# Output projection of a hybrid decoder block: two column blocks against seven quadrant products

## The chip, the cores and the metric

The kernel is one program on one core of a Trainium2 chip. Time is the device time of the core in microseconds (us); the kernel before has a median of 1022.34 us over three runs. A core has TensorE (PE, matmuls, with its weight loads as PEld), VectorE (DVE), ScalarE (ACT), GpSimd (POOL), SyncE (SP, which here only issues DMAs) and 16 DMA engines. The engines run their own instruction streams in order and wait for each other by semaphores.

## The reference, cut to what matters

```python
merged = jax.nn.sigmoid(gate_r) * y_ret + jax.nn.sigmoid(gate_m) * y_m   # (512, 1024)
x = x + merged @ w_out                # w_out (1024, 1024): the output projection, then the residual
h = rms_norm(x, norm_ffn_w)           # 512 tokens
# router logits from h: 4 groups, 32 experts; top-1 group, top-2 experts in it, their weights
# 32 experts of (silu(xb @ w_gate[e]) * (xb @ w_up[e])) @ w_down[e], D = 1024, D_EXPERT = 512, float32
# y = x + weighted sum of the two experts of each token; final rms_norm
```

## The kernel before, in words

The 512 tokens stay in SBUF. The token mixers come first, the output projection after them, then the router, then the experts.

A projection before the experts is done in float32 precision by three float32r products: a value is split into a head (`wh` of the weights, `mrgTh` of the activations, copied by ScalarE) and a tail (`wl`, `mrgTl`, value minus head, by VectorE), and TensorE adds head times head, tail times head and head times tail. Weights pass through a ring of four entries (RING). An entry is 256 rows by 512 columns, one head copy on ScalarE (`mix_head`, 128x1024) and one subtraction on VectorE (`mix_tail`, 128x1024). The heads are issued three entries ahead (LEAD).

The stages before the output projection are the five wide projections done as seven quadrant products each (FAST), and four blocks of 512 columns (`B_WR`, `B_WM`, two each) for the two branches. The second `B_WM` block ends with the gated sum `mrg` (channels by tokens, 8 tiles of 128 by 512).

The output projection is two such blocks, `B_WO` and `B_WO + 1`: each has four steps j, each step 2 halves of 2 token tiles, 2 slices of 128 rows and 3 products, so 96 matmuls of 512 columns per block and 192 in all (line 674). VectorE adds each bank to the residual `x2` (line 1690).

After the last block every token tile of `x2` is turned (`turn_stream`, 8 transposes of 128x128 each), copied to `h2T` by VectorE and ScalarE, and multiplied with the router weights (`logits`, `logit_rows`). VectorE then does the routing. TensorE meanwhile does identity matmuls that nobody reads (`stay_awake`, line 924). GpSimd gathers the tokens of the first pair of experts from a copy of `x2` in DRAM (`x_scratch`, stored by SyncE, read by an indirect DMA into `xg`), TensorE turns them (line 631) and starts the first gate product (line 956).

The experts go in 16 pairs. Each pair needs 12 chunks of weights of 1 MB (8 for gate and up, 4 for down); 192 chunks in all pass through 22 places of 8 KB per partition (`raw_moe`, plus one `guest`). SyncE issues all loads in one written order. Places that mixers and projection still use are loaded later, each behind a wait. A place is loaded a second time when TensorE has used its first chunk (`wait_chunk_used`).

## Time and profile before

| what | us |
|---|---|
| median of three runs | 1022.34 (1022.29 to 1024.7) |
| the profiled execution | 1022.9 |
| its span (first to last instruction) | 1021.0 |
| TensorE busy | 996.3 |
| VectorE, ScalarE, GpSimd busy | 500.1, 323.9, 120.8 |
| output projection on TensorE | about 491 to 534.7 |
| stream turned and router logits | 534.7 to 543.3 |
| routing, up to the first gate product | 543.3 to 561.3 |
| experts and the end | 561.3 to 1021.0 |

The span starts at the first instruction; what lies around it is 1.9 us. A busy share of 98% on TensorE says little by itself: identity matmuls count as busy too. The chain of waits tells which engine an interval hangs on. A row of the windows gives the busy time of each engine in a stretch, then the granted clock, the share of the 16 DMA engines in use, and GB/s.

### The profile page before, as it was taken

The page shows a single profiled execution, that of the slowest core. Times are in us where ns is not written, and L with a number is a line of the kernel's source. Part 1 is how long each engine was busy: PE and PEld are TensorE (multiplying, and loading weights), DVE is VectorE, ACT ScalarE, POOL GpSimd, SP SyncE. Part 2 cuts the span into 40 slices and gives each one's busy share as a digit, 9 for nine tenths or more (in the row PEclk, how much of TensorE's full clock was granted, in tenths as well). Part 3 has the DMA queues.
Part 4 walks back from the last instruction along what each step waited for, and adds up shares of the span by engine and source line. Part 5 has one row for each costly group of instructions (what it writes and reads, how often), then busy time and mean ns, then how long its engine had stood idle before and what let it go on. Part 6 is the DMA issues. An engine that isn't in the chain of part 4 may idle for free.

```text
span 1021.0 us, 13126 instructions
## 1 busy us (share of the span) xinstructions
PE 996.3 (98%) x4917; PEld 644.4 (63%) x4917; DVE 500.1 (49%) x810; ACT 323.9 (32%) x531; POOL 120.8 (12%) x152
## 2 busy tenths in 40 slices
PE   8999999999999999999998999999999999999896
PEld 7888788889889988888885333333333333333332
DVE  6268646597778677735525123333223233332235
ACT  6344535586556557622213100000000000000012
POOL 0683077000000000000000000000000000000000
PEclk9999999999999999999999999999999999999999
DMA  9223231344334525162988899999999999999993
GB/s 331 83 83 126 92 114 21 83 125 145 66 91 113 185 42 205 43 213 90 422 307 357 348 420 420 420 420 420 420 420 420 421 420 420 420 421 421 421 414 146
DMA packets 63125, 269.28 MB, mean 264 GB/s; under 512 B 9488, under 2 KB 9680, under 8 KB 38360
## 3 DMA queue, kind: packets, MB, share of 16 engines
q1 hardware_dynamic: 57464, 257.32, 63.6%
q0 software_dynamic: 5344, 11.02, 4.9%
q8 instruction: 41, 0.67, 0.3%
q14 instruction: 20, 0.16, 0.0%
q10 hardware_dynamic: 256, 0.10, 0.0%
HBM read 268.41 MB, written 4.20 MB: 267 GB/s over the span
## 4 chain that ended last, share of the span: by engine, by line
PE 72%; SPq 17%; DVE 5%; DMA 3%; ACT 2%; issue 1%; DVEq 0%; ACTq 0%
PE pj L674 23%; PE pj L854 18%; PE pj L956 12%; SPq L575 11%; PE pj L982 6%; SPq L572 6%; PE cb L631 3%; DMA raw_moe<-in_w_up_dram 3%; PE cb L992 2%; PE cb L993 1%; DVE mkT L1758 1%; DVE wl L1494 1%; PE cb L723 1%; PE cb L695 1%; ACT wh L1136 1%
## 5 line engine op out<-in xcount | busy, mean ns | idle before, releaser
L956 PE MATMUL pj<-raw_moe,xT 128*64 128x512 f32 x1016 | 227.6, 595 | 4.2 <-DMA raw_moe<-in_w_up_dram 2.4
L1494 DVE TENSOR_TENSOR wl<-raw_mix,wh 128x1024 fp32r<-128x1024 f32 x116 | 146.2, 1262 | 130.9 <-ACT wh L1136 130.6
L1970 DVE TENSOR_TENSOR x<-x,cb 128x512 f32<-128x512 f32 x120 | 77.0, 683 | 190.2 <-PE cb L993 190.2
L956 PEld LDWEIGHTS pj<-raw_moe,xT 128*64 128x64 f32 x1016 | 72.1, 137 | 140.8 <-issue 140.8
L1136 ACT ACTIVATE wh<-raw_mix 128x1024 fp32r<-128x1024 f32 x116 | 122.4, 1057 | 111.4 <-PE pj L674 68.5
L982 PE MATMUL pj<-raw_moe,hf 128*64 128x512 f32 x512 | 116.7, 598 | 1.6 <-ACT hf L1440 1.6
L982 PEld LDWEIGHTS pj<-raw_moe,hf 128*64 128x64 f32 x512 | 34.6, 136 | 67.2 <-issue 67.0
L1445 ACT ACTIVATE yh<-pj,now 128x512 fp32r<-128x512 f32 x32 | 20.4, 683 | 157.6 <-PE cb L993 143.6
L1440 ACT ACTIVATE hf<-cb 128x512 f32<-128x512 f32 x16 | 9.6, 598 | 146.3 <-PE cb L631 146.3
L992 PE MATMUL cb<-yh,hot 128*128 128x512 f32 x124 | 55.2, 445 | 0.0
L674 PE MATMUL pj<-wh,hTh 128*128 128x512 f32 x128 | 50.8, 397 | 1.7 <-DVE hTl L1525 0.7
L1975 DVE TENSOR_TENSOR xT<-cb,nwc 128x512 f32<-128x512 f32 x32 | 21.9, 687 | 58.0 <-PE cb L631 58.0
L674 PE MATMUL pj<-wl,hTh 128*128 128x512 f32 x128 | 49.9, 390 | 0.0
L674 PE MATMUL pj<-wh,hTl 128*128 128x512 f32 x128 | 49.9, 390 | 0.0
L993 PE MATMUL cb<-yl,hot 128*128 128x512 f32 x124 | 49.2, 397 | 0.0
L1436 ACT ACTIVATE sg<-pj,now 128x512 f32<-128x512 f32 x16 | 11.0, 688 | 100.7 <-PE pj L956 90.0
L992 PEld LDWEIGHTS cb<-yh,hot 128*128 128x128 f32 x124 | 23.6, 190 | 29.0 <-issue 26.2
L854 PE MATMUL pj<-wh,hTh 128*128 128x512 f32 x96 | 39.0, 406 | 0.7 <-DVE mva L1811 0.7
L854 PE MATMUL pj<-wl,hTh 128*128 128x512 f32 x96 | 37.6, 391 | 0.0
L854 PE MATMUL pj<-wh,hTl 128*128 128x512 f32 x96 | 37.4, 390 | 0.0
L854 PE MATMUL pj<-hTh,wh 128*128 128x256 f32 x128 | 36.5, 285 | 0.0
L1986 DVE SCALAR_TENSOR_TENSOR sg<-pj,now,sg 128x512 f32<-128x512 f32 x16 | 12.0, 751 | 49.5 <-PE pj L956 49.5
(397 smaller groups left out, 1858.5 us busy)
## 6 DMA issues: line engine op xcount, KB each, us to landing
raw_moe<-in_w_gate_dram SPq DMA_DIRECT2D x64, 1024.0 KB, 26.7
raw_moe<-in_w_down_dram SPq DMA_DIRECT2D x64, 1024.0 KB, 26.7
raw_moe<-in_w_up_dram SPq DMA_DIRECT2D x63, 1024.0 KB, 26.0
raw_mix<-in_w_in_dram SPq DMA_DIRECT2D x31, 1024.0 KB, 5.3
raw_mix<-in_w_in_dram POOLq DMA_DIRECT2D x10, 512.0 KB, 5.8
raw_mix<-in_w_ret_branch_dram SPq DMA_DIRECT2D x4, 1024.0 KB, 5.8
raw_mix<-in_w_mlstm_branch_dram SPq DMA_DIRECT2D x4, 1024.0 KB, 5.5
raw_mix<-in_w_out_dram SPq DMA_DIRECT2D x4, 1024.0 KB, 5.1
```

The lines of the kernel that those rows point to most:

```text
L572: sp.dma_start(weights_of(m)[:, :, :].rearrange("p (f c) n -> p f (c n)", f=2), w_down[0][e].rearrange("(a p f) n -> p a f n", a=2, f=2)[: ...
L575: sp.dma_start(weights_of(m)[:, :, :], (w_gate, w_up)[kind][0][e].rearrange("(a p k) n -> p a k n", a=2, k=4)[:, half, :, :]).then_inc(lan ...
L631: return nc.tensor.transpose(o, i, kc[0:k, K_IDENT:K_IDENT + k])
L674: m = nc.tensor.matmul(pj[:, i, :], lhsT, rhs, start=k == 0 and n == 0, stop=k == KD - 1 and n == 2)
L854: m = nc.tensor.matmul(o, lhsT, rhs, start=u in (U_11, U_21, U_T1) and k == 0 and c == 0 and n == 0, stop=k == 3 and n == 2, skip_group_ch ...
L956: mm = nc.tensor.matmul(pj[a * CAP:(a + 1) * CAP, up, :], xT[:, 4 * half + k, a * CAP:(a + 1) * CAP], weights_of(m + a)[:, k, :], start=ha ...
L982: mm = nc.tensor.matmul(pj[a * CAP:(a + 1) * CAP, 2 + c, :], hf[:, 2 * half + f, a * CAP:(a + 1) * CAP], weights_of(m + a)[:, 2 * f + c, : ...
L992: nc.tensor.matmul(bank, hot[:, t * P:(t + 1) * P], yh[:, c * 512:(c + 1) * 512], start=begin, stop=False)
L993: return nc.tensor.matmul(bank, hot[:, t * P:(t + 1) * P], yl[:, c * 512:(c + 1) * 512], start=False, stop=True)
L1136: nc.scalar.activation(wh[:, q % RING, :, :], entry_source(q), ACT.Copy).then_inc(wh_ok, 1)
L1494: V.tensor_tensor(wl[:, q % RING, :, :], entry_source(q), wh[:, q % RING, :, :].bitcast(F32), ALU.subtract).then_inc(wl_ok, 1)
L1970: V.tensor_tensor(part, part, cb[:, 2 + g % 2, :], ALU.add).then_inc(c_add, 1)
```

## The change

The output projection is written as seven products of quadrants, as the FAST projections already are. A quadrant of the activations is 512 channels by 256 tokens, one of the weights 512 by 512. With seven products in place of eight there are 7 x 2 x 4 x 3 = 168 matmuls of 512 columns. The sums that this needs are all on VectorE: four of activations (`out_part_sum`), eight of half weight quadrants (`out_weight_sum`), and 14 additions into `x2` (two for each product; ScalarE copies the `U_T1` product out first). Heads and tails of activations are now seven parts of 128x1024. The upper left weight quadrant and the upper right one get their own loads into places 12 and 13 of `raw_moe`; the right one is loaded there and again into `raw_mix`, so w_out comes in five loads of 1 MB instead of four. The expert chunks of places 12 and 13 move behind the projection. The turning of token tiles 0 and 1 and half of the logits move between the last products. The places 10, 11, 18, 19 of `raw_moe` change addresses among themselves.

```diff
-                    if b == B_WO:
-                        pe.wait_ge(mgl_ok, 2 * j + 2)
+            def out_half(u, s):
+                if u == U_11:
+                    pe.wait_ge(*out_free(s, 0))
+                if u == U_21:
+                    pe.wait_ge(*out_free(2 + s, 0))
+                if u == U_22:
+                    pe.wait_ge(tr_h, 2 * KD + s + 1)
+                if u in (U_T2, U_T3, U_T4):
+                    pe.wait_ge(*out_free(s, (U_T2, U_T3, U_T4).index(u) + 1))
+                if s == 0:
+                    pe.wait_ge(mgl_ok, (1, 3, 4, 5, 6, 2, 7)[u])
...
+            for u in range(PRODUCTS):
+                for s in range(2):
+                    out_half(u, s)
+                    if u == U_T3:
+                        turn_stream(s)
+                    if u == U_T4 and s == 0:
+                        pe.wait_ge(wrt_ok, 1)
+                        logits(0)
+            turn_stream(2)
+            logit_rows(0)
+            turn_stream(3)
             logits(1)
-            logit_rows(0)
             logit_rows(1)
...
+                    if b == B_WM + 1 and j >= 2:
+                        out_weight_sum(U_T3, j - 2)
+                    if b == B_WM + 1 and j == 3:
+                        out_weight_sum(U_T2, 0)
+                        out_weight_sum(U_T2, 1)
...
+            for x in range(2 * PRODUCTS):
+                if x in (9, 10):
+                    upper_right_last(x - 9)
+                if x in (11, 12):
+                    lower_right_last(x - 11)
+                    stream_turned(x - 11)
+                if x == 13:
+                    lower_left(0)
+                if x == 0:
+                    out_part_tail(2)
+                if OUT0 + x + LEAD < ENTRIES:
+                    mix_tail(OUT0 + x + LEAD)
+                if x == 0:
+                    out_part_sum(2)
+                    out_part_tail(3)
+                    out_part_sum(3)
+                if x in (1, 2):
+                    first_sum(x - 1)
+                if x in (3, 4):
+                    out_part_tail(x + 1)
+                if x == 5:
+                    second_sum(0)
+                    second_sum(1)
+                    out_part_tail(6)
+                if x in (6, 7):
+                    out_weight_sum(U_T4, x - 6)
+                if x == 9:
+                    router_weights()
...
-            moe_chunk(13, 0, False)
-            moe_chunk(14, 0, False)
...
-            for m in (2, 3, 5, 6):
+            for m in (2, 3, 5):
                 moe_chunk(m, 0, False)
-            sp.wait_ge(mgl_ok, KD)
-            moe_chunk(7, 0, False)
+            sp.wait_ge(mgl_ok, 7)
             moe_chunk(8, 0, False)
...
             for t in range(TT):
-                sp.wait_ge(free[t], free_of(t, BLOCKS - 1))
+                sp.wait_ge(*tile_ready(t))
                 sp.dma_start(x_dram[t * P:(t + 1) * P, :], x2[:, t, :]).then_inc(st_in, 16)
+                if t == 1:
+                    sp.wait_ge(wl_ok, out_entry(U_T4, 1) + 1)
+                    moe_chunk(14, 0, False)
+                    sp.wait_ge(*out_full(U_T3, 1))
+                    for m in (15, 17, 11, 12):
+                        moe_chunk(m, 0, False)
```

The first place is VectorE at the end of the second `B_WM` block and at the start of the projection. `wl` rows are tails of weight entries, `sgm` rows read and free the four banks, `mrg` rows are the gated sum, `mrgTl` rows are tails of it. Before:

```order
L1494 TENSOR_TENSOR wl<-raw_mix_114,wh 128x1024
L1683 TENSOR_TENSOR sgm<-pj,sgm 128x512 x4
L1696 TENSOR_TENSOR mrg<-mrg,sgm 128x512 x2
L1587 TENSOR_TENSOR mrgTl<-mrg,mrgTh 128x512
L1696 TENSOR_TENSOR mrg<-mrg,sgm 128x512
L1587 TENSOR_TENSOR mrgTl<-mrg,mrgTh 128x512
L1696 TENSOR_TENSOR mrg<-mrg,sgm 128x512
L1587 TENSOR_TENSOR mrgTl<-mrg,mrgTh 128x512 x2
L1494 TENSOR_TENSOR wl<-raw_mix_114,wh 128x1024
```

The same place now (`e5f`, `s2f` and `e3f` are sums of activations, `e5l` a tail):

```order
L1637 TENSOR_TENSOR wl<-raw_mix_126,wh 128x1024
L1759 TENSOR_TENSOR raw_mix_124<-raw_mix_124,raw_mix_125 128x1024
L1759 TENSOR_TENSOR raw_moe_109<-raw_moe_110,raw_mix_125 128x1024 x2
L1866 TENSOR_TENSOR sgm<-pj,sgm 128x512
L1868 TENSOR_TENSOR mrg<-mrg,sgm 128x512
L1866 TENSOR_TENSOR sgm<-pj,sgm 128x512
L1868 TENSOR_TENSOR mrg<-mrg,sgm 128x512
L1866 TENSOR_TENSOR sgm<-pj,sgm 128x512
L1868 TENSOR_TENSOR mrg<-mrg,sgm 128x512
L1866 TENSOR_TENSOR sgm<-pj,sgm 128x512
L1868 TENSOR_TENSOR mrg<-mrg,sgm 128x512
L1736 TENSOR_TENSOR e5f<-mrg 128x1024
```

Three weight sums now stand between the last tail of `B_WM` and the row that frees the first bank, each bank's `mrg` stands right behind its `sgm`, and sums and tails of parts (the last row is the first of them) follow before the ring's next tail.

The second place is VectorE in the middle of the projection, between the second product and the fifth. Before, between two tails of weight entries, stood the four additions of the first block:

```order
L1494 TENSOR_TENSOR wl<-raw_mix_113,wh 128x1024
L1690 TENSOR_TENSOR x_112<-pj,x_112 128x512 x4
L1720 TENSOR_TENSOR wrt<-wrt,nwc 128x8x36
L1721 MEMSET wrt 128x8x28
L1722 TENSOR_TENSOR fold<-kc 128x64
L1494 TENSOR_TENSOR wl<-raw_mix_113,wh 128x1024
```

Now:

```order
L2092 TENSOR_TENSOR x_123<-x_123,pj 128x512 x2
L1770 TENSOR_TENSOR mrgTl<-mrg,mrgTh 128x4x256
L1637 TENSOR_TENSOR wl<-raw_moe_109,wh 128x1024
L1759 TENSOR_TENSOR raw_moe_110<-raw_moe_109,raw_mix_126 128x1024
L1637 TENSOR_TENSOR wl<-raw_mix_124,wh 128x1024
L1759 TENSOR_TENSOR raw_moe_110<-raw_moe_109,raw_mix_126 128x1024
L2097 TENSOR_TENSOR x_123<-x_123,t1c 128x512 x2
L1637 TENSOR_TENSOR wl<-raw_mix_124,wh 128x1024
L2102 TENSOR_TENSOR x_123<-x_123,cb 128x512 x2
L2108 TENSOR_TENSOR x_123<-x_123,pj 128x512
L1637 TENSOR_TENSOR wl<-raw_moe_110,wh 128x1024
```

Line 2108 is the row that frees the first bank for the product `U_T3`; everything above it comes first.

The third place is SyncE's queue around the stores of `x_scratch`. Before:

```order
L575 DMA raw_moe_102<-in_w_up_dram 128x2048
L604 DMA x_scratch<-x_112 128x1024 x4
L575 DMA raw_moe_101<-in_w_up_dram 128x2048
L575 DMA raw_moe_103<-in_w_up_dram 128x2048
L575 DMA raw_moe_104<-in_w_up_dram 128x2048
L572 DMA raw_moe_105<-in_w_down_dram 128x2048
```

Now:

```order
L672 DMA x_scratch<-x_123 128x1024 x2
L616 DMA raw_moe_110<-in_w_gate_dram 128x2048
L616 DMA raw_moe_111<-in_w_gate_dram 128x2048
L616 DMA raw_moe_113<-in_w_up_dram 128x2048
L613 DMA raw_moe_107<-in_w_down_dram 128x2048
L616 DMA raw_moe_108<-in_w_gate_dram 128x2048
L672 DMA x_scratch<-x_123 128x1024 x2
L616 DMA raw_moe_112<-in_w_up_dram 128x2048
```

Five chunks of 1 MB now stand between the stores of tiles 0 and 1 and those of tiles 2 and 3, which the gather waits for.

## Rows read from the trace of the kernel before

**Rows 1.** The page's first line.

```profile
span 1021.0 us, 13126 instructions
```

**Rows 2.** Chain of waits, 484 to 580: start, length, what.

```profile
483.93 50.78 PE pj L674 x224
534.71 1.93 PE cb L631 x16
536.63 1.94 PE pj L631 x16
538.57 3.60 PE cb L900 x32
542.17 1.16 PE cb L909 x8
...
552.81 4.14 PE pj L924 x6
...
558.01 1.91 PE pj L924 x4
559.92 0.48 PE cb L631 x4
...
561.27 13.97 PE pj L956 x64
```

**Rows 3.** Windows: busy time of each engine, granted clock, DMA share, GB/s.

```profile
495.00:507.00 12.00, 12.00 (x55) 9.94 (x54) 5.59 (x7) 3.77 (x5) 0.00 (x0) 1.00 1.01 419
507.00:519.00 12.00, 12.00 (x55) 9.94 (x54) 5.62 (x9) 2.12 (x2) 0.00 (x0) 1.00 0.82 329
...
555.00:561.00 6.00, 5.87 (x48) 3.23 (x46) 1.50 (x7) 1.49 (x2) 0.53 (x1) 0.96 0.68 235
561.00:567.00 6.00, 5.73 (x28) 2.43 (x30) 0.72 (x2) 0.00 (x0) 1.03 (x1) 1.00 0.28 67
...
579.00:900.00 321.00, 318.80 (x1445) 124.02 (x1441) 99.43 (x158) 30.12 (x47) 16.62 (x36) 1.00 1.01 420
```

**Rows 4.** TensorE's timeline, 950 to 962, with the idle time before each.

```profile
951.14 3.65 PE L956 MATMUL pj<-raw_moe,xT 128*64 128x512 f32 x16 [1.32 <-DMA raw_moe<-in_w_gate_dram]
956.13 3.66 PE L956 MATMUL pj<-raw_moe,xT 128*64 128x512 f32 x16 [1.33 <-DMA raw_moe<-in_w_up_dram]
```

**Rows 5.** VectorE's timeline, 484 to 545.

```profile
486.93 1.22 DVE L1494 TENSOR_TENSOR wl<-raw_mix,wh 128x1024 fp32r<-128x1024 f32 x1 [4.21 <-ACT wh L1136]
488.08 1.28 DVE L1683 TENSOR_TENSOR sgm<-pj,sgm 128x512 f32<-128x512 f32 x2
...
497.36 2.36 DVE L1494 TENSOR_TENSOR wl<-raw_mix,wh 128x1024 fp32r<-128x1024 f32 x2 [0.25 <-ACT wh L1136]
```

**Rows 6.** Groups of VectorE by line and form, 300 to 491.

```profile
L1654 DVE TENSOR_TENSOR raw_mix<-raw_mix,raw_mix 128x1024 f32<-128x1024 f32 x13 | 15.8, 1219 | 0.0
```

**Rows 7.** ScalarE's timeline, 533 to 543.

```profile
538.19 1.07 ACT L1407 ACTIVATE squares<-x 128x1024 f32<-128x1024 f32 x1
539.13 0.21 ACT L1407 ACTIVATION_READ_ACCUMULATOR squares<-x 128x1 f32 x1
539.23 0.60 ACT L1412 ACTIVATE h2T<-pj 128x512 f32<-128x512 f32 x1
```

**Rows 8.** DMA issues: number, KB each, median us from issue to landing.

```profile
x_scratch<-x SPq DMA_DIRECT2D x4, 512.0 KB, 7.2
...
xg<-x_scratch,tok_now POOLq DMA_INDIRECT x14, 8.3
...
xg<-x_scratch,tok_tab POOLq DMA_INDIRECT x2, 4.1
```

**Rows 9.** SyncE's timeline, 430 to 640.

```profile
531.38 4.40 SPq L604 DMA_DIRECT2D x_scratch<-x  x4
...
556.02 9.34 SPq L572 DMA_DIRECT2D raw_moe<-in_w_down_dram  x2
```

**Rows 10.** GpSimd's timeline, 540 to 625.

```profile
554.13 1.40 POOL L2171 DMA_INDIRECT xg<-x_scratch,tok_tab  x1 [183.70 <-DVE cnt L2020]
```

**Rows 11.** Window of the routing stage.

```profile
543.40:561.30 17.90, 15.31 (x96) 7.54 (x96) 11.68 (x49) 3.37 (x6) 1.40 (x1) 0.90 0.87 338
```

More of the change, by code:

```diff
@@ L421, in entry_used, with out_entry, out_place, out_full @@
             return pair_used, 3 * F0 + PRODUCTS * len(FAST) + 3 * (b - B_WR) + j + 1
+        def out_entry(u, v):
+            return OUT0 + 2 * u + v
+        out_slot = {U_11: 12, U_T1: 13, U_T2: 12, U_T4: 13}
+        OUT_SUM = {U_T1: 1, U_T3: 4, U_T2: 6, U_T4: 11}
+        ROW_SUM = (3, 8, 9, 10)
+        def out_place(u):
+            return raw_moe[out_slot[u]] if u in out_slot else raw_mix[slot_of(2 * B_WO + (U_T3, U_22, U_21).index(u))]
+        def out_full(u, s):
+            if u in (U_T1, U_22):
+                return tr_ps, 2 * KD + (2 if u == U_22 else 0) + s + 1
+            if u == U_21:
+                return full[2 + s], full_of(2 + s, B_WM + 1) + 1
+            return full[s], full_of(s, B_WM + 1) + (U_11, U_T2, U_T3, U_T4).index(u) + 1
+        def out_free(s, n):
+            return free[s], free_of(s, B_WM + 1) + n
+        def tile_ready(t):
+            return out_free(t % 2, 2 + t // 2 * 2)
+        def stream_bank(t, half):
+            return cb[:, 2 * t + half, :] if t < 2 else pj[:, 6 - 2 * t + half, :]
         def half_before(x):
@@ L476, in mix_chunk @@
                     w, c0 = w_in[0], IN_COLS[b]
-                else:
-                    w, c0 = (w_ret, w_mlstm, w_out)[(b - B_WR) // 2][0], 512 * (b % 2)
+                elif b < B_WO:
+                    w, c0 = (w_ret, w_mlstm)[(b - B_WR) // 2][0], 512 * (b % 2)
                 m = n - 2 * B_WR
@@ L488, in mix_chunk @@
                     sp.wait_ge(wl_ok, fast_entry(len(FAST) - 1, U_T4 if m else U_T3, 1) + 1)
+                if n >= 2 * B_WO:
+                    half, c0, w = ((0, 512), (1, 512), (1, 0))[n - 2 * B_WO] + (w_out[0],)
                 sp.dma_start(raw_mix[slot_of(n)][:, :, :],
@@ L767, in block_of @@
             def block_of(b):
[L768 removed]
+                act = (hTh, hTl) if b < B_WR else (retTh, retTl) if b < B_WM else (mixTh, mixTl)
                 if b == B_RK:
@@ L885, in turn_stream @@
             def turn_stream(t):
-                pe.wait_ge(free[t], free_of(t, BLOCKS - 1))
+                pe.wait_ge(*tile_ready(t))
+                if t == 0:
+                    pe.wait_ge(tr_l, 2 * KD + 4)
+                if t == 2:
+                    for i in (2, 3):
+                        pe.wait_ge(*out_free(i, 1))
                 for half in range(2):
-                    bank = cb[:, 2 * t + half, :] if t < 2 else pj[:, 2 * t + half - TT, :]
                     for k in range(4):
-                        m = turn(bank[:, k * P:(k + 1) * P], x2[:, t, 512 * half + k:512 * (half + 1):4])
+                        m = turn(stream_bank(t, half)[:, k * P:(k + 1) * P], x2[:, t, 512 * half + k:512 * (half + 1):4])
                     m.then_inc(h2T_ps, 1)
@@ L1313, in block_of @@
                         root(3 + b - B_WR, 8)
+                    if b == B_WM + 1 and j < 2:
+                        out_part_head(j)
             def fast_evict(p, u, s):
```

287 lines of the change are left out of this document (214 added, 73 removed).

## The prediction, blind

> **What bounds the kernel now.** I read the page, the chain of waits, the windows and the timelines of single engines, in that order. The span is 1021.0 us [rows 1]. From 484 to 543.3 the chain is TensorE without a break: the projection, 16 + 16 transposes, the logits, the logit rows; each piece starts where the last ends [rows 2]. 224 matmuls take 50.78 us, so one takes 0.2267 us, and the 192 of the projection take 43.5 us: it starts at 534.7 - 43.5 = 491.2. The reader should see that VectorE is less than half busy there (5.6 of 12 us) [rows 3]. From 543.3 the chain is small VectorE work and identity matmuls, and at 559.92 the first gathered tokens are turned [rows 2].
>
> From 579 to 900 TensorE is busy, but the DMA engines are also full, at 420 GB/s [rows 3]. A chunk of 1.049 MB then takes 2.50 us, a pair's twelve 30.0 us. TensorE needs less than that per pair and eats up its lead of 22 places; at 951 and 956 it waits for chunks, 1.3 us each [rows 4]. So both limits meet near the end. To finish earlier the kernel must start the experts earlier **and** the stream of chunks must get ahead. The slack of the stream is one hole: at 561 to 567 the DMA engines are used at 0.28 (67 GB/s), because all places are full and the next load waits for a first use [rows 3]; SyncE's row with two issues from 556.02 lasts 9.34 us, so the second is issued near 565.0 [rows 9].
>
> **TensorE's work.** 24 matmuls fewer, 24 x 0.2267 = -5.4 us. Transposes, logits and rows are as many as before; moving them costs nothing by itself.
>
> **VectorE's work.** A 128x1024 tail costs 1.14 us in a row of them (2.36 for two, less 1.22) [rows 5]; a 128x1024 sum has the same length, 1219 ns [rows 6]. A 128x512 addition costs 0.60 in a row (1.28 for two, less 0.68) [rows 5]. Strided 4x256 forms are not in the trace as tails; I take them at the 128x1024 price, nearest in size. The engine's queue, followed through the changed order:
>
> - The last `B_WM` tail starts at 486.93, the next instruction could start at 488.08 [rows 5]. Three weight sums are now in front of the four banks: 3 x 1.14, so 491.5. The first bank is free at 492.2 instead of before 491.2: TensorE waits **1.1**.
> - The gated sum now stands behind each bank and waits for its own predecessor: 4 x (0.60 + 0.60 + 0.14) = 5.4, to 496.9. One part sum and one tail later, at 499.3, the second product may start; TensorE is done with the first at 492.3 + 5.4 = 497.7. It waits **1.7**.
> - Third product: its first weight tail is seventh in the queue, 496.9 + 7 x 1.14 = 505.0, about when TensorE comes (499.4 + 5.4 = 504.8); the next tail is behind a bank addition. Together **0.8**.
> - The product `U_T3` needs bank 0, freed by the first `U_T2` addition. From 496.9 to its end stand 3 part sums, 5 part tails, 9 weight tails, 2 weight sums and 9 additions: 19 x 1.14 + 9 x 0.60 = 27.1, with waits for its own results 524.3. TensorE could be there at 499.4 + 4 x 5.44 + 0.8 = 522.0. It waits **2.3**.
>
> VectorE thus works without a pause from 486.9 to about 528, and waits of 5.9 us take the place of 5.4 saved.
>
> **The end of the projection.** From 524.3: four halves of 2.72 (10.9), turns of tiles 0 and 1 (1.9), half the logits (1.8): 538.9. Then turn, rows, turn (0.97 + 0.3 + 0.97): 541.1. The second half of the logits waits for ScalarE, which after tile 2 is turned (539.9) does copy, square, copy: 0.5 + 1.2 + 0.6 [rows 7], 542.3; TensorE waits 1.2, then 1.8 for the logits and 0.9 for copy and rows: 545.3 where it was 543.33 [rows 2]. **Routing starts 2.0 us later.** Bounds: if ScalarE's chain overlaps the turn fully, 1.2 less; if each 4x256 tail cost a tenth more, 0.8 more.
>
> **SyncE's queue.** Chunks of places 12 and 13 came early; now nothing is issued from about 492 until the seventh part tail. Its place in VectorE's queue is 14 x 1.14 + 4 x 0.60 after 496.9, near 515.5. Before, the engines were full or at 0.82 in this time [rows 3]. Behind it wait 17 chunks (42.5 us), 2.1 MB of stores (5) and the token row (0.6): about 48 us from 517.6, so full to about 566. Before, the last of these had landed soon after 561 (share 0.68, then 0.28) [rows 3]. Two things hang on it.
>
> The **stores** of tiles 2 and 3 stand behind five chunks (12.5 us). In the trace the four stores follow one another within 4.40 us [rows 9] and land 7.2 us after issue [rows 8]. Now tile 3's is issued near 539.8 and lands near 552. The gather comes at 554.13 + 2.0 = 556.1 [rows 10]: covered, but only by 4 us. Without the stalls of VectorE this would be the next bound.
>
> The **gather** runs beside a full queue. The first two, beside an emptying queue, landed after 4.1 us (median), the other fourteen, with the stream full, after 8.3 [rows 8]. At 554.13 + 4.7 (the first of the two is the longer; the window's half empty share speaks for no more) TensorE was still in its identity matmuls, which end at 559.92 [rows 2]: 0.9 us of cover. Now 556.1 + 8.3 = 564.4 against 559.92 + 2.0 = 561.9: **2.5 to 2.7 more**. Bounds: 0 (4.1 as before) and 4 (9.5 us of backlog ahead of it).
>
> The Trainium skill (DMA: Bandwidth & Descriptors, Queues, rings and completion order) says that a DMA engine alternates between queue rows packet by packet. By that rule the gather shares with the chunks and doesn't stand behind them. The rows with 8.3 us agree with sharing; were it one line, the sum would be 1.5 us larger.
>
> **Experts.** The first gate product begins at 561.27 + 4.7 = 566.0, the first place is free near 569.7, after the queue has run dry (566), so the stream starts as much later as TensorE does. Both limits that met at 951 move by the same amount, nothing absorbs it. The fifth load of w_out (2.5 us) falls into the hole before 517 and costs nothing; without the hole it would be 2.5 us of the stream.
>
> **Sum.** -5.4 + 5.9 + 1.2 + 0.3 for the order of the last rows = +2.0; gather +2.7; **+4.7** in all. The profiled execution has 1022.9 us (1.9 more than its span) and would become 1027.6; on the median of 1022.34 the same step gives **1027.0**.
>
> **Rivals.**
>
> 1. *The gather doesn't feel the queue.* Everything else holds, +2.0: 1024.4. For it: the backlog is only 10 us deep, not 26. Against: 8.3 in all fourteen busy cases. Chance 0.18.
> 2. *VectorE keeps up and TensorE's 5.4 us arrive.* Then routing would start 4 us earlier. It doesn't end there: tile 3's store lands near 550, the gather is 3.6 slower, and the chunks still need 48 us from the seventh tail, which comes some 3 us earlier; the first gate product comes 0 to 1 us earlier, 1021.8. Chance 0.12. It is faster by over 0.3%, at 1017, only if the chunks also get through early: the hole between 492 and 517 must then not exist. It decides at the point where the seventh part tail is done before 505. Together with all that I overlooked, 0.05.
> 3. *The clock falls in the gather's wait.* In the routing stage the granted clock has a mean of 0.90, and three doubled identity matmuls take 4.14 us where two later take 1.91 [rows 2, 11]. Before that fall TensorE had small work with gaps. Now it waits 2.6 us for the gather; if the clock is at 1.2 GHz in the first 4 us of the gate product, 1.7 more: 1028.7. Chance 0.15. The Trainium skill (TensorE: Matmul & The Clock Gate, Part 1) has the gate follow recent activity; this trace shows one such fall, none after a wait as short as this.
> 4. *Slower still:* 4x256 forms a tenth dearer and the stores behind the gather, 1030. Chance 0.05.
>
> Forecast itself: 0.45. A change of 0.3% is 3.07 us; this is about what a measurement of this kernel tells from none. Above 1025.4 lie the forecast's cases but for its lower edge, 3 and 4; between, the lower edge, 1 and most of 2. Slower 0.70, same 0.24, faster 0.06. Range 1021.8 to 1030.2; the likeliest case alone 1025.3 to 1029.
>
> **What would show it.** Right: VectorE busy over 90% from 487 to 528; TensorE idle about 1, 1.7, 0.8 and 2.3 us at the starts of the products 1, 2, 3 and 6; DMA share near 0 for ten microseconds around 510, then full to 566; first `xg` gather landing after 8 us and TensorE idle before line 705's `xg` rows. Wrong: a projection of 38 us without gaps; a gather of 4 to 5 us; the DMA engines full before 515; or a steady stream that catches up later and leaves the end where it was.

## The result and the profile after

The changed kernel takes 1033.27 us (median of five, 1029.1 to 1033.86) where the kernel before takes 1022.34: 10.9 us more. The ratio is 1.0085, with a 95% interval of 1.006 to 1.0109. A second series of the same kernel (`e18_after_again`) gave 1033.22 against 1023.11, ratio 1.0095 (1.0079 to 1.011). Two of the five executions took only 1029.1 and 1029.5, so the means, 1031.9 and 1023.2, are 8.6 us apart, less than the medians. So it is slower, as forecast, but by about twice the 4.7 us of the forecast, and the median is above its range; those two executions are inside it.

The profiled execution is the median one. The page's first line, to [rows 1]:

```profile
span 1031.4 us, 13137 instructions
```

The chain of waits from 484 on (start, length, what), to [rows 2]:

```profile
498.19 0.85 DVE mrgTl L1770
499.25 1.22 DVE wl L1637
...
524.27 4.61 PE pj L1015 x12
...
533.56 2.77 PE pj L1015 x12
536.33 1.88 PE cb L976 x16
538.21 2.96 PE pj L1015 x12
...
546.85 0.65 PE cb L985 x4
...
558.29 9.69 DMA xg<-x_scratch,tok_tab
...
569.71 15.64 PE pj L1071 x64
```

Four readings. The part from 491 to 524 has turned from TensorE into VectorE work: VectorE is busy for 40.5 of the 41 us from 487 to 528. The first half of product 6, twelve matmuls, takes 4.61 us from 524.27 while a like one later takes 2.77. The gather of the first tokens is now in the chain, 9.69 us long. The first 64 gate matmuls take 15.64 us; before, 13.97 [rows 2]. They start at 569.71 in place of 561.27.

The windows (busy time of PE, PEld, DVE, ACT, POOL, then granted clock, DMA share, GB/s), to [rows 3, 11]:

```profile
503.00:518.00 15.00, 14.80 (x64) 11.52 (x63) 15.00 (x16) 10.00 (x11) 0.00 (x0) 1.00 0.09 22
518.00:531.00 13.00, 11.24 (x46) 8.78 (x45) 11.05 (x16) 4.48 (x7) 0.00 (x0) 0.87 1.00 413
...
556.00:562.00 6.00, 5.63 (x22) 2.35 (x22) 3.48 (x18) 1.46 (x2) 1.41 (x1) 0.50 1.02 419
562.00:568.00 6.00, 3.57 (x37) 1.91 (x36) 0.00 (x0) 0.03 (x1) 0.00 (x0) 0.93 0.83 336
568.00:574.00 6.00, 5.50 (x22) 2.50 (x24) 1.29 (x2) 0.00 (x0) 1.03 (x1) 0.72 0.11 31
```

VectorE has no pause from 503 to 518, and the DMA engines stand nearly still there (22 GB/s; 329 in 507 to 519 before, [rows 3]). From 518 to 566 they are full (in the row from 562 on, 1.0 up to 566, then 0.65 and 0.28 in the last two us). TensorE's granted clock is below 1 in three places of this part: 0.87 in 518 to 531 means 3.4 of the 13 us at 1.2 GHz, 0.50 in 556 to 562 all six (before: 0.90 over the whole routing stage), and 0.72 in 568 to 574 another 3.4 us, now under the first gate products.

The timelines of TensorE and GpSimd around the waits, to [rows 2, 10]; in brackets the idle time before and who ended it:

```profile
492.28 0.50 PE L1015 MATMUL pj<-wh,mrgTh 128*128 128x512 f32 x1 [1.04 <-DVE sgm L1866]
...
524.27 0.50 PE L1015 MATMUL pj<-wh,mrgTh 128*128 128x512 f32 x1 [1.76 <-DVE x L2108]
...
568.11 1.21 PE L705 MATMUL cb<-kc,xg 128*128 128x128 f32 x8 [2.54 <-DMA xg<-x_scratch,tok_tab]
```

```profile
558.29 1.41 POOL L2432 DMA_INDIRECT xg<-x_scratch,tok_tab  x1 [187.78 <-DVE cnt L2281]
```

And SyncE's, to [rows 9]: the load of the second round is issued at 575.5 (560.19 + 15.28, end of a row with two issues) where it was issued at 565.4.

```profile
515.57 1.46 SPq L613 DMA_DIRECT2D raw_moe<-in_w_down_dram  x2
...
537.08 5.16 SPq L672 DMA_DIRECT2D x_scratch<-x  x2
...
560.19 15.28 SPq L613 DMA_DIRECT2D raw_moe<-in_w_down_dram  x2
```

At the end of the experts nothing has been made up; the waits for chunks of [rows 4] stand 10 us later:

```profile
961.58 3.65 PE L1071 MATMUL pj<-raw_moe,xT 128*64 128x512 f32 x16 [1.62 <-DMA raw_moe<-in_w_gate_dram]
966.54 3.65 PE L1071 MATMUL pj<-raw_moe,xT 128*64 128x512 f32 x16 [1.31 <-DMA raw_moe<-in_w_up_dram]
```

### The profile page after: what moved, and what is told of

It reads as the page before. It is cut to its first block, busy times and chain, and to the rows that moved or that the text cites. A ratio compares the mean times of both kernels' runs of the same rounds, so it can differ in the third digit from the quotient of the medians.

```text
span 1031.4 us, 13137 instructions
## 1 busy us (share of the span) xinstructions
PE 998.3 (97%) x4893; PEld 641.2 (62%) x4893; DVE 526.6 (51%) x833; ACT 333.2 (32%) x538; POOL 120.8 (12%) x152
## 4 chain that ended last, share of the span: by engine, by line
PE 67%; SPq 17%; DVE 8%; DMA 4%; issue 2%; ACT 2%; DVEq 0%; POOLq 0%; POOL 0%; ACTq 0%
PE pj L926 18%; PE pj L748 18%; PE pj L1071 12%; SPq L616 11%; PE pj L1097 6%; SPq L613 6%; DMA raw_moe<-in_w_up_dram 3%; PE cb L705 3%; DVE wl L1637 2%; PE cb L1107 2%; PE cb L1108 1%; PE pj L1015 1%; DMA xg<-x_scratch,tok_tab 1%; DVE mkT L1923 1%; ACT wh L1251 1%
## 5 line engine op out<-in xcount | busy, mean ns | idle before, releaser
L1637 DVE TENSOR_TENSOR wl<-raw_mix,wh 128x1024 fp32r<-128x1024 f32 x114 | 143.7, 1261 | 116.8 <-ACT wh L1251 116.4
```

What stands on the lines that cost most here:

```text
L1637: V.tensor_tensor(wl[:, q % RING, :, :], entry_source(q), wh[:, q % RING, :, :].bitcast(F32), ALU.subtract).then_inc(wl_ok, 1)
```

## Experiments

All were timed in five rounds beside the kernel before, whose median was 1023.1 to 1023.4 in these series. "Rows end" is the end of the last logit row, where routing starts (543.3 before, 547.5 after).

### Pauses of TensorE and its clock: e1_awake

The changed kernel with small matmuls of ones, which nobody reads, ahead of three waits:

```diff
+            def filler(n):
+                for _ in range(n):
+                    nc.tensor.matmul(cb[:, 3, 0:P], onesq[:, :], onesq[:, :], start=True, stop=True)
             def out_half(u, s):
+                if s == 0:
+                    filler({U_11: 4, U_21: 5, U_T3: 7}.get(u, 0))
```

> The changed kernel, with 4, 5 and 7 small matmuls that nobody reads (128x128 of ones) put ahead of TensorE's waits for the products 1, 2 and 6. Nothing else moves. Theory A (TensorE's waits in the projection make the clock fall to 1.2 GHz at 525.3, which costs 1.9 us): the granted clock stays at 1.00 from 500 to 550, the half product after 524.3 takes 2.7 us instead of 4.6, the routing starts near 545.7 instead of 547.5, the time is 1.5 to 2 us shorter (1031 to 1032) and the five runs lie closer together. Rival (the fall is not tied to these waits, or comes elsewhere then): the fall is still there and the time is that of the changed kernel, 1029 to 1034.

Measured: 1029.87 us (1029.13 to 1031.61), ratio 1.0071 (1.0057 to 1.0085). The median is 3.4 us below that of the changed kernel, more than the 1.5 to 2 us expected, although the matmuls do nothing. The ratios of the two kernels lie closer (1.0085 and 1.0095 without the matmuls) and their intervals overlap. What speaks for an effect is the single times: seven of the nine of the changed kernel, in two series, are above 1031.8, and none of these five is. The profiled execution is the shortest of the five. Its chain:

```profile
524.24 3.02 PE pj L1022 x12
...
545.24 0.65 PE cb L985 x4
...
556.68 8.89 DMA xg<-x_scratch,tok_tab
...
567.31 13.97 PE pj L1078 x64
```

Product 6 starts at the same moment as without them (524.2), so VectorE's queue is as long as it was; only the speed behind the wait has changed: 3.02 in place of 4.61. Rows end at 545.9, 1.6 us earlier. The gather takes 8.9 us, the gate products run at full speed. The edit does not touch that place, so these 1.7 us at the gate are not shown to be its work.

### The late queue and the gather: e4_quiet, e5_before_late

e4_quiet is the changed kernel with four chunks (places 15, 17, 18, 19) held back until the first gather has landed:

```diff
-            for m in (16, 18, 19, 20):
-                moe_chunk(m, 0, False)
             sp.wait_ge(lg_ps, 2)
             moe_chunk(GUEST, 0, False)
+            sp.wait_ge(gat, 16)
+            for m in (16, 18, 19, 20):
+                moe_chunk(m, 0, False)
```

> The changed kernel, but the four chunks of places 15, 17, 18, 19 are issued only after the first gather has landed; token row and guest chunk go before. Theory A (the gather is slow, 9.7 us instead of 4.7, because the queue is full beside it): the queue is dry near 556, the gather issued at 558.3 lands near 563, the gate product starts after the identity matmuls, near 567 instead of 569.7, and since the four chunks now fill the hole before the first reuse of a place, the end moves by the same 2.5 to 4 us, to 1029 to 1031. Rival B (the stream decides): four chunks 7 us later put the stream off, the time is 1035 or more. Rival D (the gather is slow for another reason, its store or the indirect addressing): it still takes over 8 us and the time is that of the changed kernel or worse.

Measured: 1032.92 us (1032.34 to 1033.72), ratio 1.0098 (1.0083 to 1.0114). The gather, issued at 556.6, landed after 4.6 us, TensorE did not wait for it, and the first gate product began at 563.9, 5.8 us earlier than in the changed kernel (1.6 of it because the clock did not fall in the projection of this execution). The time is between the cases expected, 1029 to 1031 and 1035 or more. Nothing of the gain reached the end: TensorE now waits for chunks eight times, 9.3 us in sum, from 868.7 on (three times and 4.0 us in the changed kernel).

```profile
868.67 3.65 PE L1072 MATMUL pj<-raw_moe,xT 128*64 128x512 f32 x16 [0.56 <-DMA raw_moe<-in_w_gate_dram]
873.63 3.65 PE L1072 MATMUL pj<-raw_moe,xT 128*64 128x512 f32 x16 [1.30 <-DMA raw_moe<-in_w_up_dram]
```

So the full queue is what makes the gather long, and holding chunks back only moves the price into the stream.

e5_before_late is the kernel before, projection and all, with the two chunks whose places the change takes for w_out issued behind the stores:

```diff
-            moe_chunk(13, 0, False)
-            moe_chunk(14, 0, False)
...
-            for m in (16, 18, 19, 20):
+            for m in (13, 14, 16, 18, 19, 20):
```

> The kernel before, with the chunks of places 12 and 13 (two loads of 1 MB) issued behind the stores of the tokens instead of before the projection: SyncE's part of the change alone, in small. Theory A: the queue is full until about 561, so the first gather at 554.1 takes 8 us or more instead of 4.7 and lands near 562.5; the gate product starts 2.5 to 3.5 us later than 561.3, maybe with a fall of the clock behind the wait (1.7 more); time 1025 to 1027. Rival (the two chunks fill the hole of the DMA engines at 561 to 567 and nobody waits for them): time as before, 1022.3.

Measured: 1028.32 us (1027.58 to 1028.53), ratio 1.0048 (1.0034 to 1.0062). Rows end at 543.4 as before, and yet 4.9 us are lost against its kernel before, 1.3 us past the upper end of what was expected:

```profile
554.00 8.64 DMA xg<-x_scratch,tok_tab
...
564.75 15.83 PE pj L954 x64
```

The gather takes 8.6 in place of 4.7 us, TensorE waits 3.8 for it, and its clock is at 1.2 GHz after that wait: 15.83 in place of 13.97. Two megabytes later in one queue cost half of what the whole change does. The matmuls at the gate are slow here behind a projection without a pause, so the clock's fall there does not need the waits of the projection.

### VectorE's weight sums: e3_light, e7_pool6

e3_light cuts each of the eight weight sums to one column. The products then use wrong weights, and the routing that follows from them led to a second round of the experts (28 later gathers in the trace in place of 14), so its total (1514.98 us) says nothing and only the trace up to the first gate product is read.

```diff
-                V.tensor_tensor(dst, one, two, ALU.add).then_inc(sum_ok, 1)
+                V.tensor_tensor(dst[:, :, 0:1], one[:, :, 0:1], two[:, :, 0:1], ALU.add).then_inc(sum_ok, 1)
```

> The changed kernel with the eight weight sums cut to one column of each row, so the products work on wrong weights; what is left out is 8 x about 1 us of VectorE. Theory A (VectorE's queue makes TensorE wait 4.9 us and the clock falls after it): no waits over 0.5 us in the projection, U_T3 starts near 518.5 instead of 524.3, no fall of the clock there, routing starts near 539.8 instead of 547.5. The end does not follow in full: the seventh part tail comes only 3.4 us earlier, so chunks fill the DMA engines until about 563, the gather takes 9 to 10 us and the first gate product starts near 562 to 563; time 1024 to 1026, still not below the kernel before. Rival B (the stream of chunks decides alone, whatever TensorE does): first gate product earlier, but the time within 2 us of the changed kernel, 1030 or more. Rival C (TensorE's time was all): 1033.3 - 7.7 = 1025.6 without the gather's share, and below 1022 if the gather is short.

Measured: no wait in the projection, rows end at 541.6 (1.7 earlier than before, 1.8 later than expected). But the gather, issued at 552.4, landed after 9.2 us, TensorE waited 3.5 for it, and the first gate product began at 563.7, still 2.4 later than before:

```profile
561.70 1.96 PE L705 MATMUL cb<-kc,xg 128*128 128x128 f32 x8 [3.52 <-DMA xg<-x_scratch,tok_tab]
```

Seven products that VectorE's weight sums do not hold up would have given nothing here, with SyncE's order as it is.

e7_pool6 moves six of the eight sums (`U_T3`, `U_T2`, `U_T4`) to GpSimd, which is idle then:

```diff
+            for u in (U_T3, U_T2, U_T4):
+                for v in range(2):
+                    pool_weight_sum(u, v)       # two adds of 128x512 each
             pool.wait_ge(st_in, 16 * TT)
```

> The changed kernel with the weight sums of T3, T2 and T4 on GpSimd (six of eight), nothing else. VectorE is 6 x 1.2 us freer, so products 2, 3 and 6 no longer wait; if the fall of the clock at 525.3 follows these waits it is gone, the last row ends at 542.5 to 544 (547.5 in the changed kernel), the gather still takes 8 to 9.5 us beside the queue, TensorE's clock falls once more in the gather's wait, and the time is 1027 to 1029. If TensorE's clock falls anyway, it is 1030 to 1033.

Measured: 1030.22 us (1030.0 to 1030.96), ratio 1.0071 (1.0058 to 1.0084), above the 1027 to 1029 expected. No fall of the clock in the projection, rows end at 545.0 where 542.5 to 544 was expected. That is 0.9 earlier than with VectorE alone and no fall; 6 x 1.14 = 6.8 us of work had left VectorE. VectorE's and GpSimd's timelines of this run tell where it went:

```profile
501.95 1.22 DVE L1641 TENSOR_TENSOR wl<-raw_moe,wh 128x1024 fp32r<-128x1024 f32 x1
503.08 0.68 DVE L2083 TENSOR_TENSOR x<-x,pj 128x512 f32<-128x512 f32 x1
503.68 1.94 DVE L1641 TENSOR_TENSOR wl<-raw_moe,wh 128x1024 fp32r<-128x1024 f32 x1
...
506.14 1.71 DVE L1641 TENSOR_TENSOR wl<-raw_mix,wh 128x1024 fp32r<-128x1024 f32 x1
507.78 2.31 DVE L1772 TENSOR_TENSOR e3l<-e3f,e3h 128x1024 fp32r<-128x1024 f32 x1
510.01 2.31 DVE L1641 TENSOR_TENSOR wl<-raw_mix,wh 128x1024 fp32r<-128x1024 f32 x1
```

```profile
503.25 7.99 POOL L2430 TENSOR_TENSOR raw_moe<-raw_moe,raw_mix 128x512 f32<-128x512 f32 x4 [15.40 <-DVE wl L1641]
```

While GpSimd adds, four subtractions on VectorE take 1.94, 1.71, 2.31 and 2.31 us in place of 1.22: 3.4 us go back. The account is closed with it: the gated sum starts at 489.6 in place of 491.6 (three sums fewer ahead of it, but the tail before it now waits for ScalarE's head), two sums further on are 2.3 us more, and 2.0 + 2.3 - 3.4 = 0.9. The additions that read a bank (0.68) are not longer. The Trainium skill (SBUF — State Buffer, Who interferes with whom) says that a VectorE instruction with two SBUF inputs contends with a GpSimd instruction that reads SBUF. The rows agree: GpSimd's additions are longer too, 2.0 us each (7.99 for four) where two at 479.76 took 3.46 together. They don't show that one stands still for the whole of the other.

### The clock in the gather's wait: e10_late_wake, e13_pool_wake, e15_wake

Small matmuls ahead of the turn of the gathered tokens, in three kernels: ten in e5_before_late (e10), eight in e7_pool6 (e13), ten in the changed kernel (e15).

```diff
             stay_awake(2)
+            wake(10)
             first_gate(0)
```

> The kernel before with the chunks of places 12 and 13 issued behind the stores (its run alone gave 1028.3, first gate product at 564.8, clock at 1.2 GHz from 561.7 for 6.8 us) and ten small matmuls ahead of the wait for the gather. If the clock that falls in that wait is part of the price, it stays at 2.4 GHz at the first gate products and the time is 1026 to 1027; the rest, 3 to 4 us over the kernel before, is then the gather beside the queue. If the late chunks cost only by their stream, the time stays at 1028.

Measured: 1027.29 us (1026.35 to 1028.25), ratio 1.0037 (1.0023 to 1.0051), against 1.0048 without them. The wait for the gather is 1.95 in place of 3.81; the clock still falls, but 2.7 us later, and is at 1.2 GHz for 3.4 us in place of 6.8. The first gate product stays where it was (564.7), since the gather takes 9.0. The time is 0.3 above the 1026 to 1027 expected; the gain of 1 us is within the intervals of the two kernels, so it is not shown.

> The same with eight small matmuls ahead of the gather's wait: against the run with the six sums on GpSimd alone it parts the clock in that wait from the gather beside the queue. If the clock is priced as elsewhere, it gives back 1.5 to 2 us, so 1025.5 to 1027; the queue's 4 us stay. If the gather alone decides, the two are equal.

Measured: 1029.5 us (1027.94 to 1030.34), ratio 1.0058 (1.0045 to 1.0071); the gather took 9.8, the wait for it was still 3.2, the gate matmuls took 15.45. The 1025.5 to 1027 expected did not come: against e7_pool6 it is 0.7 us less, not told apart from none, and the clock fell with the eight matmuls too, 3.1 us later and for 3.4 us in place of 6.8.

> The changed kernel with ten small matmuls ahead of the wait for the gather alone; the projection is as in the changed kernel, its clock fall at 525 too. Of the 3.4 us that the matmuls ahead of products 1, 2 and 6 gave (1033.3 to 1029.9), this tells which part belongs to the gate's clock: if the fall at the first gate products costs 1.7 us, the time is 1031 to 1032; if the price was all in the projection, it stays at 1033.

Measured: 1031.5 us (1029.67 to 1034.37), ratio 1.0086 (1.0072 to 1.0099). The times spread over 4.7 us. The profiled one is a short one (1029.9). Its projection has the waits of the changed kernel, with nothing edited there, and no fall of the clock:

```profile
524.31 0.50 PE L1015 MATMUL pj<-wh,mrgTh 128*128 128x512 f32 x1 [1.74 <-DVE x L2109]
...
566.34 1.20 PE L705 MATMUL cb<-kc,xg 128*128 128x128 f32 x8 [1.45 <-DMA xg<-x_scratch,tok_tab]
```

```profile
518.00:531.00 13.00, 11.26 (x53) 9.07 (x52) 11.00 (x16) 5.03 (x8) 0.00 (x0) 1.00 1.00 405
```

The fall in the projection, then, happens in some executions and not in others. e4_quiet's trace, with the same projection, has none either. So of the four traces with this projection and no matmuls in its waits, two have the fall (the changed kernel's and e18_after_again's) and two do not; the profiled run of e1_awake alone does not tell its effect from chance.

### Which wait, and is it by chance: e17_fill6, e18_after_again

```diff
-                    filler({U_11: 4, U_21: 5, U_T3: 7}.get(u, 0))
+                    filler({U_T3: 7}.get(u, 0))
```

Of e1_awake's matmuls, e17 keeps only those ahead of product 6 (the diff is against e1_awake), and it has the ten at the gather of e15_wake; e18 is the changed kernel without an edit.

> The changed kernel with seven small matmuls ahead of product 6 (the wait of 1.76 us at 524.3) and ten ahead of the gather's wait; products 1 and 2 wait as before. If the clock in the projection falls for the wait of product 6 alone, the times are 1028.5 to 1030.5 with none above 1032. If it falls for the sum of the waits, some of the five runs are still at 1032 to 1034, as with the ten alone.

Measured: 1030.69 us (1029.14 to 1031.31), ratio 1.007 (1.0056 to 1.0083). No time above 1031.4; with the ten alone, three of the six that e15 gave were. Rows end at 546.0, and the clock stays up in the projection though the waits ahead of products 1 and 2 are as long as in the changed kernel. That points at the wait ahead of product 6, but it is not shown: the intervals of e15 and e17 overlap, and e15's own trace has no fall either. The clock fell at the gate here, ten matmuls or not.

> The changed kernel once more, without an edit. Its five times stood at 1029.1, 1029.5, 1033.3, 1033.6 and 1033.9, and the trace with the clock's fall at 525.3 is one of the long ones. If that fall happens in some executions and not in others, the times part again in two groups about 4 us apart, and a trace of the short group shows no fall in the projection and the last row at 545.8 to 546. If the fall is always there, the cause of the two groups is elsewhere and a short trace shows it too.

Measured: 1033.22 us, four times from 1031.88 to 1034.3, ratio 1.0095 (1.0079 to 1.011). The short group did not come back, so the two groups are not shown on this kernel again. The granted clock over each execution says something of them: the two short ones of the first series had a mean of 0.994, its three long ones 0.988 to 0.991, and the four here 0.990 to 0.993. They differ in how long the clock was down. The kernel before spreads with it too, from 1021.98 us at 0.997 to 1024.78 at 0.993 in the series beside e1_awake, so not all of the spread belongs to the change. The profiled time, the longest, has the fall once more (row one), and the one at the gate (row two):

```profile
524.99 4.42 PE pj L1015 x12
...
570.73 15.65 PE pj L1071 x64
```

### How much is the queue: e11_less, e12_before_less

In both, half of each of the chunks m = 14 to 19 is not loaded in the first round (3.1 MB), and their products read the loaded half twice, so the output isn't the reference's. e11 is e1_awake with this edit, e12 the kernel before.

```diff
-                    sp.dma_start(weights_of(m)[:, :, :], ...[:, half, :, :])
+                    ks = slice(0, 2 if not used and m in (14, 15, 16, 17, 18, 19) else 4)
+                    sp.dma_start(weights_of(m)[:, ks, :], ...[:, half, ks, :])
```

> The changed kernel with the small matmuls ahead of products 1, 2 and 6 (1029.9 without more), and with half of each of the chunks m = 14 to 19 left out in the first round (3.1 MB less, about 8.6 us of the queue at 363 GB/s; the products of the second pair of experts read the loaded half twice, so the output is not the reference's). If the queue that VectorE's sums leave late is what delays the experts, the queue has run dry by about 559, the gather takes 5 to 6 us in place of 8.9, the first gate product starts at 562.5 to 564 in place of 567.3 and the time is 1024 to 1026. If the stream of chunks sets the end by its bytes alone, the time falls by the whole 8.6, to 1021. If neither, it stays at 1029 to 1030.

> The same halves left out in the kernel before (output not the reference's). Its queue is dry at 554 and its slots are full when the first gate product starts, so if it has no shortage of chunks the time stays within 1 us of 1022.5; if its stage of experts is set by the stream's bytes, it falls by up to 8.6 us, to 1014 to 1015. That result is the scale against which the run of the changed kernel with these halves left out is read.

Measured: e11 1025.56 us (1024.34 to 1027.27, eleven runs), ratio 1.0025 (1.0016 to 1.0034); e12 1023.2, ratio 0.9999 (0.999 to 1.0008). So the bytes alone are worth nothing in the kernel before, and 4.3 us in the changed one (1029.87 - 1025.56). The intervals of e11_less and e1_awake do not overlap. The windows of e11 and its chain:

```profile
550.00:556.00 6.00, 3.80 (x37) 1.65 (x36) 5.02 (x22) 0.20 (x1) 0.00 (x0) 1.00 1.02 422
556.00:562.00 6.00, 5.52 (x48) 3.21 (x47) 2.27 (x12) 1.49 (x2) 1.41 (x1) 1.00 0.61 219
```

```profile
562.79 13.97 PE pj L1079 x64
```

The DMA engines run dry while the gather is under way; issued at 556.5, it landed at 560.8, under the identity matmuls, and the gate product starts at 562.8 instead of 567.3.

### Does a later start carry over: e16_before_fill

```diff
             stay_awake(2)
+            wake(18)
             first_gate(0)
```

> The kernel before with eighteen small matmuls (0.22 us each) ahead of the turn of the gathered rows: nothing else moves, and the first gate product starts 4 us later, at 565.3. In the traces so far the span is the start of the first gate product plus 459.7 to 460.1 where the clock stays up, whichever kernel it is; if the experts' stage is an unbroken stream that begins there, this run takes 1027 us. If the stream has slack to make up the delay, it takes 1023 to 1025.

Measured: 1026.39 us (1026.28 to 1028.14), ratio 1.0035 (1.0021 to 1.0049), 3.3 us over its kernel before. In the profiled execution (1028.14, the longest; it is 0.9 late from the start of the program on, where the clock was down for 3.4 us) the first gate product is at 566.3 and the span 1026.3: 5.0 and 5.3 us later than in the kernel before. The stage of experts has no slack. All traces but e3_light's beside one another, us:

```
kernel                first gate product   span     difference   clock at the gate
before                561.3                1021.0   459.7        full
e12_before_less       561.4                1021.5   460.1        full
e16_before_fill       566.3                1026.3   460.0        full
e11_less              562.8                1022.5   459.7        full
e1_awake              567.3                1027.3   460.0        full
e15_wake              567.9                1028.0   460.1        full
e10_late_wake         564.7                1026.0   461.3        fell
e13_pool_wake         567.1                1028.4   461.3        fell
e17_fill6             567.5                1028.8   461.3        fell
e7_pool6              566.7                1028.4   461.7        fell
e18_after_again       570.7                1032.4   461.7        fell
after                 569.7                1031.4   461.7        fell
e5_before_late        564.8                1026.6   461.8        fell
e9_pool_awake         565.9                1027.9   462.0        fell
e14_pool_wake_hold    563.6                1025.9   462.3        full, 2 chunks held back
e4_quiet              563.9                1030.5   466.6        full, 4 chunks held back
```

The time is the start of the first gate product plus 460, plus 1.3 to 2.0 where the clock is down there, plus what the stream lacks where chunks come late.

### Attempts at a better version: e9_pool_awake, e14_pool_wake_hold

e9 is e7_pool6 with the matmuls of e1_awake and eight at the gather. e14 is e13_pool_wake with places 18 and 19 issued after the gather has landed.

> The changed kernel with three edits: the weight sums of T3, T2 and T4 go to GpSimd (six of the eight that VectorE does), products 1, 2 and 6 have small matmuls of ones ahead of their waits, and eight more stand ahead of the wait for the gather. If the loss were made in the projection (VectorE's sums and the clock), the last row would end at about 543 as in the kernel before, the first gate product would start at 562 to 563 and the time be 1023 to 1025. If most of it is SyncE's order (chunks issued late, the gather behind a full queue), the row ends at 543 to 545, but the gather still takes 8 to 9 us beside the chunks, the first gate product starts at 565 to 567, and the time is 1027 to 1029.

Measured: 1027.97 us (1027.26 to 1029.72), ratio 1.0045 (1.0031 to 1.0059). No wait in the projection at all, rows end at 545.3, gather 8.0: the second of the two cases foreseen.

> The same again with two of the six late chunks (places 18 and 19, 2.1 MB, 5.8 us of the queue) issued only when the gather has landed. By the queue's account the gather lands 2 to 4 us sooner and the first gate product starts at 561 to 563; if two chunks held back don't leave the experts short, the time is 1022.5 to 1025, no worse than the kernel before. If the bytes then come too late, as with four held back, TensorE waits for chunks in the experts by about what it won, and the time is 1027 to 1030.

Measured: 1028.65 us (1027.79 to 1029.64), ratio 1.0057 (1.0044 to 1.0069). The gather landed after 6.4 and the gate product began at 563.6, but TensorE then waited for chunks five times, 5.8 us (three and 3.8 in e13). No version with the seven products came to the kernel before. The hole of the DMA engines from 503 to 518 is common to all of them, and the bytes missed there have to come when the gather wants the engines, or later, when the experts want them. A version in which SyncE has something to load in that hole was not run.

## Why the prediction was wrong in size

The direction and the path were right; three terms were too small, one of them taken as nothing, and a fourth stood only as an unlikely rival. Of the 10.4 us of span:

| step | forecast | trace |
|---|---|---|
| rows end, clock up | +2.0 | +2.6 (e1_awake, e15_wake) |
| clock falls at product 6 | not named | +1.6 (547.5 against 545.9) |
| gather behind its cover | +2.7 | +4.2 (8.4 less 4.2) |
| clock at the first gate products | rival 3: +1.7, chance 0.15 | +2.0 (461.7 against 459.7) |
| sum | +4.7 | +10.4 |

**TensorE's work, VectorE's work.** These held. The waits ahead of products 1, 2, 3 and 6 were forecast as 1.1, 1.7, 0.8 and 2.3 us and are 1.04, 1.39, 0.20 and 1.76, together 4.4 in place of 5.9. That product 6, forecast at 524.3, starts at 524.27 is VectorE's queue read rightly; that the loss before it comes out as 5.8 is partly luck, since the 120 matmuls of the first five products took 28.6 us and not 27.2, about what the waits fell short. VectorE worked without a pause, and the loss ate the saving of 24 matmuls.

**The end of the projection.** It was to be 545.3 and was 547.5. With the clock up it is 545.9, so the working was 0.6 short: the four halves took 11.5 us (3.02, 2.78, 2.77, 2.96) and not 10.9; ScalarE's wait was 0.91, not 1.2, but a further 0.48 stood ahead of the rows. (Walked piece by piece, the prediction's own terms end at 545.0; the 545.3 comes from its sum.) The other 1.6 is the step that failed first: after 524.3 I priced every matmul at 0.2267 us, as if TensorE's clock did not care for the pauses put before it. I had looked for the clock in the gather's wait alone (rival 3). In the profiled execution it fell at 525.3, 1.0 us after the wait of 1.76. e15_wake and e4_quiet show that it doesn't happen each time. With matmuls in the wait of product 6 no trace of three has the fall (e1_awake, e11_less, e17_fill6) and no time of e1_awake and e17_fill6 is above 1031.7; that fits the waits as its cause, and does not prove it.

**SyncE's queue.** The hole was forecast from 492 to 515.5 and full engines to 566; SyncE issues again at 515.57, and the engines are full until 566. e12_before_less shows that the kernel before had room for these bytes, e11_less that the changed one has not.

**The gather.** Its issue came 4.2 us late, as rows end did. I took 8.3 us, the median of the fourteen gathers in the steady stream [rows 8], as if all had it; in the trace of before they lie between 7.9 and 9.7. This one took 9.69. This term is the second step that failed, 4.2 in place of 2.7. Beside a full queue the first gather took 8.0 to 9.8 in the eleven traces that have one. Less the cover, that is just past the upper bound of 4 that I gave. In the changed kernel and in e5_before_late it lands just when the engines fall idle (share 0.65 in 566 to 567, 0.28 in 567 to 568, landed at 567.97), which looks like standing in line. It isn't: in e7_pool6 the engines are full to 567 and the gather lands at 564.5 after 8.9 us, in e9_pool_awake at 564.2 after 8.0. The length hangs on whether the engines are full, little on how much stands ahead. The Trainium skill's rule (DMA: Bandwidth & Descriptors, Queues, rings and completion order), that an engine alternates between the queues it has work for, agrees with these traces.

**Rival 3** was right and got a chance of 0.15, because the trace of before showed "none after a wait as short as this". It had no such wait at all (its longest for chunks are 1.3 us): absence was read as evidence. Of the nine traces of timed kernels with a wait of 1.67 us or more for the gather, with matmuls ahead or not, eight took 15.1 to 15.8 us for the first 64 gate matmuls; e1_awake, with 1.71, took 13.97, and so did e15_wake with 1.45 (13.98). The length of the wait is not all of it: e9_pool_awake, with 1.67, took 15.67. In e1_awake and e15_wake the clock had already fallen and come back under the identity matmuls of the routing, where it costs nothing; in the six of the eight that are neither the changed kernel nor its second run it had stayed up there until after 561. The granted clock of e1_awake (row one) and e9_pool_awake (row two):

```profile
556.00:562.00 6.00, 6.00 (x38) 2.61 (x36) 2.44 (x12) 1.49 (x2) 1.41 (x1) 0.56 1.01 416
556.00:562.00 6.00, 5.52 (x52) 3.49 (x51) 1.67 (x10) 1.49 (x2) 1.16 (x1) 1.00 1.00 417
```

The changed kernel, with waits of 2.54 and 3.93 us in its two traces, has both falls. What decides between one and two is not shown.

**Experts.** "Nothing absorbs it" was right, as e16_before_fill shows. The range ended at 1030.2 because the clock terms and the gather's bound were never added together. The forecast's own cases, rival 3's 1.7 and the gather's upper bound of 4 in place of 2.7, already give 1030.0; the fall at product 6, for which it had no term, brings that past the range.

What the pieces are worth in medians: 1033.2 to 1029.9 with matmuls in the waits (e1; the least sure step), to 1025.6 for the queue beside the gather (e11), and 2.4 to the kernel before for a projection that ends later in spite of 24 matmuls fewer. Open is why the clock falls in one execution and not in the next with the same waits, and so how much of the first step is the edit's work.

## What to carry to other kernels

When a change turns one unbroken stretch of TensorE work into the same stretch with pauses, price the matmuls behind each pause at both levels of the clock, and let the range reach to the sum of these prices. Ask what a scratch buffer taken from a later stage's weights does to the order of loads: two chunks issued late cost 5 us with nothing else changed, through one small gather beside a full queue. Where a stream-bound stage follows, its start plus a constant can be the time (460 us here), and work saved ahead of it counts only if both the first product and the queue are early.

## What the runs showed of the hardware

- With matmuls that nobody reads put into its waits, a kernel that starts its products no earlier had a median 3.4 us shorter (e1_awake; the intervals of the ratios overlap). Twelve matmuls of 512 columns, for 3.4 us of them at 1.2 GHz, took 4.4 to 4.6 us, at 2.4 GHz 2.8 to 3.0.
- With the same instructions and the same waits (1.0, 1.4, 1.75 us within 32 us) the clock fell in two traces and stayed up in two others.
- The same gather, issued by GpSimd, takes 4.4 to 4.8 us when the load queue runs empty or stands, and 8.0 to 9.8 beside a full one.
- A two-input float32 VectorE instruction of 128x1024, alone 1.22 us, takes 1.7 to 2.3 while GpSimd adds from SBUF (e7_pool6); one of 128x512 that reads PSUM stays at 0.68.
